# First x tile ahead of the weights, and activation sums rounded one unit sooner, in a one-core macaron decoder layer

## The chip, the core and the metric

The kernel runs on one NeuronCore of a Trainium2 chip. Its engines are TensorE (PE, with its weight loads shown apart as PEld), VectorE (DVE), ScalarE (ACT), GpSimd (POOL) and SyncE (SP), each with its own instruction stream; they meet only at semaphores. Loads from memory are issued on the queue of SP, and some on ACT's. The metric is the time of one execution in microseconds (us); less is better.

## What is computed

One layer of a decoder: a SwiGLU feed-forward, a mixer of two attention branches, and a second feed-forward, each between a norm ahead and a norm behind. The change lies in the two feed-forwards.

```python
def swiglu(x, w_gate, w_up, w_down):
    return (jax.nn.silu(x @ w_gate) * (x @ w_up)) @ w_down
...
    f1 = swiglu(rmsnorm(h, ffn1_pre_g[l]), ffn1_w_gate[l], ffn1_w_up[l], ffn1_w_down[l])
    h = h + 0.5 * rmsnorm(f1, ffn1_post_g[l])
...
    f2 = swiglu(rmsnorm(h, ffn2_pre_g[l]), ffn2_w_gate[l], ffn2_w_up[l], ffn2_w_down[l])
    h = h + 0.5 * rmsnorm(f2, ffn2_post_g[l])
```

There are 512 tokens, 1024 features and 2816 hidden features, all in float32.

## The kernel before

**Three products for one.** Each float32 operand is split in two: ACT writes a rounded copy (`w_hi`, `u_hi`, `a_hi`, and the first half of `tc`), DVE subtracts it from the original and writes the rest (`w_lo`, `u_lo`, `a_lo`, the second half of `tc`). PE then makes three matmuls: hi times hi, hi times lo, lo times hi. A unit is 128x1024 weights; four slots of `raw`, `w_hi` and `w_lo` go round.

**The start.** The first feed-forward starts from x transposed, in eight tiles of 128 features by 512 tokens (`xt`, which lies in `arena`). ACT makes `u_hi` of a tile with the gain `g1` (`u_tile`), DVE makes `u_lo` (`u_pair`). Units 0 and 1 are the first columns of w_gate and w_up. Each comes in two loads: the part for features 0 and 1 (`first_part(j, 0, 2)`, semaphore `w0_in[j]`) and the rest (`first_part(j, 2, KD)`). SP issues these four, then units 2 and 3 (`first_load`), then x in token order into `h`. ACT issues the gain and all of x transposed: tiles 0 and 1 one by one (L520), the other six in three loads of two (L522). All that stands ahead of ACT's first rounding (`first_hi(0)`, L706), which waits for `w0_in[0]`. PE goes by pairs of tiles (`earliest_units`, L1606 to L1612): for each of four pairs the six matmuls of unit 0 and the six of unit 1, so it needs tile pair n and, from pair 1 on, the rest of both weights. On ACT the order is first_hi(0), tiles 0 and 1, first_hi(1), rest_hi(0), tiles 2 and 3, rest_hi(1), tiles 4 to 7, units 2 and 3. Behind units 0 to 3 PE spreads the norm's factors with one matmul (L1622); ACT copies them (L652).

**The classic units and the pairs.** Units 0 to 7 are plain (`CLASSIC`); unit j is read from its bank by `silu` (ACT, L660) where j is even, with a scaling by DVE ahead of it in the first feed-forward (L1145), and by a product on DVE where j is odd (L1149, `hidden_ready`). Unit 6 takes the banks of unit 2, so PE waits for the second product of L1149 ahead of it. What follows are nine pairs (QP), each of seven units (STEPS) of half-size matmuls (L1534 to L1536): products of sums of weight blocks (DVE, L1047) and sums of activation blocks, from which the four wanted blocks are put together (`quads`, L1072). The activation sums are T_3, T_1, T_2 and T_4: DVE makes them in `token_sum` (L1129), ACT rounds them in `t_hi` (L643), DVE takes the rest in `t_lo` (L1105). They are made once for each feed-forward, and PE needs them from the second unit of the first pair on. Rounding a pair's weights is L604 on ACT, the rest L1053 on DVE.

**What sets the order.** Nothing is scheduled by a planner. Each engine's program is written out by hand, and an engine takes its rows in that order, each when its semaphores allow. In the loop over units 0 to 7 (`ffn` of ACT and of DVE) the token sums stand at units 0 to 3 and their rounding at units 4 to 7.

Of the kernel before, what the change touches and what calls it, by code (L numbers as in the profile page):

```python
# [23 lines left out]
P = 128  # L24
# [76 lines left out]
def macaron_layer(nc, h_store, x_t, g1cols, x, w1g, w1u, w1d, g1post, gmpre, w_in, b_forget, w_alpha, b_alpha,  # L101
                  gla_g, w_bf, w_bg, w_out, gmpost, g2pre, w2g, w2u, w2d, g2post, out):
    with ExitStack() as ctx:
# [295 lines left out]
        def _(sp):  # L399
# [45 lines left out]
            def first_part(j, k0, k1, done):  # L445
                src = kmajor((w1g, w1u)[j], slice(0, P))
                sp.dma_start(tiles(j)[:, k0:k1, :], src[:, k0:k1, :]).then_inc(done, 16)

            first_part(0, 0, 2, w0_in[0])
            first_part(1, 0, 2, w0_in[1])  # L450
            first_part(0, 2, KD, raw_in[0])
            first_part(1, 2, KD, raw_in[1])
# [59 lines left out]
        def _(act):  # L512
# [3 lines left out]
            act.wait_ge(bias_set, 1)  # L516
            nc.scalar.activation(ones[:, :], eps_t[:, :], ACT.Copy, scale=0.0, bias=1.0).then_inc(warm_set, 1)
            act.dma_start(g1[:, :], g1cols).then_inc(g1_in, 16)
            for k in range(2):
                act.dma_start(xt[:, k, :], x_t[k * P:(k + 1) * P, :]).then_inc(xt0_in[k], 16)  # L520
            for n in range(1, KD // 2):
                act.dma_start(xt[:, 2 * n:2 * n + 2, :],  # L522
                              x_t[2 * n * P:(2 * n + 2) * P, :].rearrange("(k p) c -> p k c", p=P)).then_inc(xt_in[n], 16)

            def split(u, i=0, per=0, second=None):

                act.wait_ge(raw_in[slot(u)], i * (16 * per // SLOTS) + arrivals(u))
                if second is not None:
                    act.wait_ge(*second)
                if not isinstance(i, int) or u + per * i >= SLOTS:  # L530
                    act.wait_ge(unit_used, i * per + (u - SLOTS + 1))
                nc.scalar.activation(w_hi[:, slot(u), :], raw[:, slot(u), :], ACT.Copy).then_inc(hi_ready, 1)  # L532
# [112 lines left out]
            def ffn(u0, layer):  # L645
                for j in range(4 * CLASSIC):
                    i, jj = j // 4, j % 4
                    if layer == 0 and j == 0:
                        split(u0 + 4)
                        split(u0 + 5)  # L650
                        act.wait_ge(rstd_spread, 1)
                        nc.scalar.activation(rstd_all, bank[:, 4, :], ACT.Copy).then_inc(rstd_kept, 1)  # L652
                    if jj % 2 == 0:
                        src = silu[:, jj // 2, :]
                        if layer:
                            act.wait_ge(unit_used, u0 + j + 1)
                            src = bank[:, classic_bank(layer, j), :]
                        else:
                            act.wait_ge(z_scaled, j // 2 + 1)
                        nc.scalar.activation(silu[:, jj // 2, :], src, ACT.Silu).then_inc(silu_ready, 1)  # L660
                    if i < CLASSIC - 1:
                        if layer:
                            split(u0 + j + 4)
                        elif jj % 2 == 0:
                            split(u0 + jj // 2 + 6)
                    else:
                        t_hi(layer, jj, (T_3, T_1, T_2, T_4)[jj])
                        pair_hi(layer, 0, jj)
                for q in range(QP):
                    for n in range(STEPS):  # L670
                        if q and n == 0:
                            silu_quads(layer, q - 1, 1)
                            silu_quads(layer, q - 1, 2)
                        if n == 1:
                            snapshot(layer, q, 0, y_pair(q))
                        if n == 2:
                            snapshot(layer, q, 1, w_pair)
                        if n == 3:
                            snapshot(layer, q, 2, y_pair(q))
                        if n == 5:  # L680
                            silu_quads(layer, q, 0)
                        if n == 0:
                            if q:
                                pair_hi(layer, q, 3)
                        elif n <= 3:
                            pair_hi(layer, q, n + 3)
                        elif q < QP - 1:
                            pair_hi(layer, q + 1, n - 4)
                        else:
                            down_hi(layer, n - 4)  # L690
                silu_quads(layer, QP - 1, 1)
                silu_quads(layer, QP - 1, 2)
                for n in range(3, KF):
                    down_hi(layer, n)
# [15 lines left out]
                nc.scalar.activation(w_hi[:, j, 2 * P:UNIT], raw[:, j, 2 * P:UNIT], ACT.Copy).then_inc(hi_ready, 1)  # L710

            first_hi(0)
            act.wait_ge(g1_in, 16)
            u_tile(0)
            u_tile(1)
# [223 lines left out]
        def _(dve):  # L939
# [191 lines left out]
            def ffn(u0, layer):  # L1131
                if layer:
                    for m in range(4):
                        token_whole(layer, m)
                for j in range(4 * CLASSIC):
                    i, jj = j // 4, j % 4
                    if layer == 0 and j == 0:
                        split(u0 + 4)
                        split(u0 + 5)
                        dve.wait_ge(rstd_kept, 1)  # L1140
                    if jj % 2 == 0 and layer == 0:
                        dve.wait_ge(unit_used, u0 + j + 1)
                        if i:
                            dve.wait_ge(hidden_ready, PAIRS + j // 2 - 1)
                        V.tensor_tensor(silu[:, jj // 2, :], bank[:, classic_bank(layer, j), :], rstd_all, ALU.mult).then_inc(z_scaled, 1)  # L1145
                    if jj % 2:
                        dve.wait_ge(unit_used, u0 + j + 1)
                        dve.wait_ge(silu_ready, 2 * CLASSIC * layer + j // 2 + 1)
                        V.tensor_tensor(arena[:, j // 2, :], silu[:, jj // 2, :], bank[:, classic_bank(layer, j), :],  # L1149
                                        ALU.mult).then_inc(hidden_ready, 1)  # L1150
                    if i < CLASSIC - 1:
                        if layer:
                            split(u0 + j + 4)
                        elif jj % 2:
                            split(u0 + jj // 2 + 6)
                        token_sum(layer, jj)
                        continue
                    t_lo(layer, jj, (T_3, T_1, T_2, T_4)[jj])
                    if jj == 0:
                        pair_sum_of(layer, 0, "S3")  # L1160
                        pair_sum_of(layer, 0, "S1")
                    pair_lo(layer, 0, jj)
                    if jj == 0:
                        pair_sum_of(layer, 0, "S2")
                    if jj == 3:
                        pair_sum_of(layer, 0, "S4")
                for q in range(QP):
                    last = q == QP - 1
                    for n in range(STEPS):
                        if n == 0 and q:  # L1170
                            if layer == 0:
                                quad_scale(q - 1, 2)
                            pair_lo(layer, q, 3)
                            pair_sum_of(layer, q, "S4")
                            quad_mul(layer, q - 1, 0)
                            quad_mul(layer, q - 1, 1)
                        if 1 <= n <= 3:
                            pair_lo(layer, q, n + 3)
                            if n == 1 and q:
                                quad_mul(layer, q - 1, 2)  # L1180
                            if n > 1 and not last:
                                pair_sum_of(layer, q + 1, ("S3", "S1")[n - 2])
                        if n >= 4:
                            quads(layer, q, n - 4)
                            if layer == 0 and n != 5:
                                quad_scale(q, n // 6)
                            if last:
                                down_lo(layer, n - 4)
                            else:
                                pair_lo(layer, q + 1, n - 4)  # L1190
                                if n == 4:
                                    pair_sum_of(layer, q + 1, "S2")
                if layer == 0:
                    quad_scale(QP - 1, 2)
                for n in range(3):
                    quad_mul(layer, QP - 1, n)
                for n in range(3, KF):
                    down_lo(layer, n)
# [738 lines left out]
```

## Time and profile before

| | us |
|---|---|
| median of 3 runs | 1090.79 |
| lowest, highest | 1090.13, 1091.5 |
| the profiled execution | 1090.27 |
| its span, first to last instruction | 1088.4 |
| PE busy | 1075.5 (99%) |
| PE weight loads busy | 957.5 (88%) |
| DVE busy | 667.9 (61%) |
| ACT busy | 503.0 (46%) |

1.9 us of the profiled execution lie outside its span, and it is 0.5 us below the median. The granted clock of TensorE is at full speed (2.4 GHz) in all of the 40 slices. PE is busy nearly throughout, so an edit can only give back one of PE's few gaps, or open one. Matmul ends are modelled, so a gap is best read from the start of a matmul behind a wait.

### The profile page before, as it was taken

To read this page: it belongs to the slowest core of one execution; us is meant where nothing else is said; L and a number is where in the kernel's file an instruction comes from. 1 tells how busy PE (TensorE), PEld (TensorE's weight loads), DVE (VectorE), ACT (ScalarE), POOL (GpSimd) and SP (SyncE) were. 2 spreads that over 40 slices of the span, in tenths; PEclk is the share of its full clock that TensorE was granted. 3 is DMA by queue.
4 is the path that set the end of the run, shared out by engine and by line. 5 is a ranking of instruction groups with operands and counts; after the bars stand their busy time and mean duration, and the time that the engine had idled before them with its cause. 6 is when DMAs were issued, how large, how long until landed. Compare 5 with 4: busy or idle time off the path is not lost.

```text
span 1088.4 us, 15986 instructions
## 1 busy us (share of the span) xinstructions
PE 1075.5 (99%) x6534; PEld 957.5 (88%) x6534; DVE 667.9 (61%) x810; ACT 503.0 (46%) x729; POOL 44.7 (4%) x96
## 2 busy tenths in 40 slices
PE   8999999999999999999999999999999999999997
PEld 6899999998888978888888888889899999988886
DVE  6898888873334663476664333468687887753334
ACT  7354455552223573667773222344445454542222
POOL 2000000000001210001000000011000000000001
PEclk9999999999999999999999999999999999999999
DMA  9522423334322544332115334315434234153311
GB/s 301 183 78 87 147 79 101 133 98 174 96 81 58 175 121 108 84 78 78 40 39 155 97 109 161 97 41 173 155 95 139 79 108 125 78 178 113 95 40 78
DMA packets 116131, 121.17 MB, mean 111 GB/s; under 512 B 6592, under 2 KB 100816, under 8 KB 116064
## 3 DMA queue, kind: packets, MB, share of 16 engines
q1 hardware_dynamic: 111744, 113.37, 33.8%
q10 hardware_dynamic: 3344, 4.20, 1.4%
q0 software_dynamic: 976, 2.66, 0.7%
q8 instruction: 47, 0.77, 0.3%
q14 instruction: 20, 0.16, 0.1%
HBM read 111.80 MB, written 6.29 MB: 108 GB/s over the span
## 4 chain that ended last, share of the span: by engine, by line
PE 90%; DVE 4%; ACT 3%; issue 1%; DMA 1%; POOL 0%; SPq 0%; ACTq 0%; DVEq 0%; POOLq 0%
PE bank L1448 25%; PE bank L1534 11%; PE bank L1536 11%; PE bank L1535 11%; PE bank L1438 7%; PE bank L1440 7%; PE bank L1439 7%; PE bank L1653 1%; PE bank L1654 1%; PE bank L1655 1%; PE bank L1503 1%; PE bank L1504 1%; PE bank L1505 1%; DMA raw<-in_ffn_w_up 1%; PE bank L1750 1%
## 5 line engine op out<-in xcount | busy, mean ns | idle before, releaser
L1534 PE MATMUL bank<-tc,w_hi 128*128 128x256 f32 x576 | 163.0, 283 | 0.0
L1535 PE MATMUL bank<-tc,w_hi 128*128 128x256 f32 x576 | 163.0, 283 | 0.0
L1536 PE MATMUL bank<-tc,w_lo 128*128 128x256 f32 x576 | 163.0, 283 | 0.0
L945 DVE TENSOR_TENSOR w_lo<-raw,w_hi 128x1024 fp32r<-128x1024 f32 x71 | 86.6, 1221 | 96.5 <-ACT w_hi L532 96.4
L1059 DVE TENSOR_TENSOR w_lo<-raw,w_hi 128x1024 fp32r<-128x1024 f32 x40 | 49.0, 1226 | 129.6 <-ACT w_hi L610 129.6
L1448 PE MATMUL bank<-w_hi,a_hi 128*128 128x512 f32 x408 | 126.1, 390 | 0.0
L1448 PE MATMUL bank<-w_hi,a_lo 128*128 128x512 f32 x408 | 125.7, 389 | 0.0
L1448 PE MATMUL bank<-w_lo,a_hi 128*128 128x512 f32 x408 | 125.6, 389 | 0.0
L1438 PE MATMUL bank<-u_hi,w_hi 128*128 128x512 f32 x312 | 124.0, 397 | 0.2 <-issue 0.2
L1534 PE MATMUL bank<-u_hi,w_hi 128*128 128x256 f32 x432 | 122.3, 283 | 0.8 <-DVE scr L1072 0.8
L1536 PE MATMUL bank<-u_hi,w_lo 128*128 128x256 f32 x432 | 122.2, 283 | 0.0
L1535 PE MATMUL bank<-u_lo,w_hi 128*128 128x256 f32 x432 | 122.2, 283 | 0.0
L1440 PE MATMUL bank<-u_hi,w_lo 128*128 128x512 f32 x312 | 121.8, 390 | 0.0
L1439 PE MATMUL bank<-u_lo,w_hi 128*128 128x512 f32 x312 | 121.6, 390 | 0.0
L1534 PEld LDWEIGHTS bank<-tc,w_hi 128*128 128x128 f32 x576 | 110.6, 192 | 0.0
L1535 PEld LDWEIGHTS bank<-tc,w_hi 128*128 128x128 f32 x576 | 110.6, 192 | 0.0
L1536 PEld LDWEIGHTS bank<-tc,w_lo 128*128 128x128 f32 x576 | 110.6, 192 | 0.0
L610 ACT ACTIVATE w_hi<-raw 128x1024 fp32r<-128x1024 f32 x40 | 42.4, 1060 | 141.6 <-PE bank L1448 137.9
L532 ACT ACTIVATE w_hi<-raw 128x1024 fp32r<-128x1024 f32 x71 | 74.7, 1054 | 56.0 <-PE bank L1440 24.3
L1448 PEld LDWEIGHTS bank<-w_lo,a_hi 128*128 128x128 f32 x408 | 76.6, 188 | 15.9
L1448 PEld LDWEIGHTS bank<-w_hi,a_lo 128*128 128x128 f32 x408 | 76.6, 188 | 15.9
L1448 PEld LDWEIGHTS bank<-w_hi,a_hi 128*128 128x128 f32 x408 | 76.1, 188 | 15.7 <-DVE arena L1408 0.2
(244 smaller groups left out, 2057.9 us busy)
## 6 DMA issues: line engine op xcount, KB each, us to landing
raw<-in_ffn_w_down SPq DMA_DIRECT2D x40, 512.0 KB, 3.6
raw<-in_w_in SPq DMA_DIRECT2D x40, 512.0 KB, 3.8
h<-in_ffn_w_gate SPq DMA_DIRECT2D x9, 1024.0 KB, 5.5
h<-in_ffn_w_up SPq DMA_DIRECT2D x9, 1024.0 KB, 8.5
raw<-in_ffn_w_gate SPq DMA_DIRECT2D x9, 1024.0 KB, 5.4
raw<-in_ffn_w_up SPq DMA_DIRECT2D x9, 1024.0 KB, 8.0
h<-in_x SPq DMA_DIRECT2D x8, 512.0 KB, 6.5
h_store<-h SPq DMA_DIRECT2D x2, 2048.0 KB, 9.3
```

Source lines behind the costliest of these rows:

```text
L532: nc.scalar.activation(w_hi[:, slot(u), :], raw[:, slot(u), :], ACT.Copy).then_inc(hi_ready, 1)
L610: nc.scalar.activation(w_hi[:, slot(u), :], raw_down(layer, n), ACT.Copy).then_inc(hi_ready, 1)
L945: V.tensor_tensor(w_lo[:, slot(u), :], raw[:, slot(u), :], w_hi[:, slot(u), :].bitcast(F32), ALU.subtract).then_inc(lo_ready, 1)
L1059: V.tensor_tensor(w_lo[:, slot(u), :], raw_down(layer, n), w_hi[:, slot(u), :].bitcast(F32), ALU.subtract).then_inc(lo_ready, 1)
L1438: mm(dst, w_hi[:, slot(u), w], rhs_hi[:, k - k0, :], start=k == k0, stop=False)
L1439: mm(dst, w_hi[:, slot(u), w], rhs_lo[:, k - k0, :], start=False, stop=False)
L1440: last = mm(dst, w_lo[:, slot(u), w], rhs_hi[:, k - k0, :], start=False, stop=k == k1)
L1448: last = mm(bank[:, 2 * t + c, :], a[:, s, toks], w[:, s, c * HALF:(c + 1) * HALF], start=first and a is a_hi and w is w_hi, stop=final an ...
L1503: mm(dst, w_hi[:, s, w], u_hi[:, k, toks], start=k == 0, stop=False)
L1534: mm(dst, w_hi[:, slot(u), w], moving(n, 0, k), start=first and k == 0, stop=False, skip_group_check=True)
L1535: mm(dst, w_hi[:, slot(u), w], moving(n, 1, k), start=False, stop=False, skip_group_check=True)
L1536: last = mm(dst, w_lo[:, slot(u), w], moving(n, 0, k), start=False, stop=k == KD // 2 - 1, skip_group_check=True)
```

## The change

The loads of x tiles 0 and 1 move from ACT's queue to SP's: tile 0 ahead of all weights, tile 1 behind the first part of w_gate. The three loads of the six later tiles stay on ACT's queue, but behind its first rounding. And the splits of the activation sums T_3, T_1 and T_2 move from units 4, 5 and 6 to units 1, 2 and 3, that of T_4 from unit 7 to unit 4, on ACT and on DVE, in both feed-forwards. No operation is added or taken away.

```diff
@@ sync
+            def first_rows(k):
+                sp.dma_start(xt[:, k, :], x_t[k * P:(k + 1) * P, :]).then_inc(xt0_in[k], 16)
+
+            first_rows(0)
             first_part(0, 0, 2, w0_in[0])
+            first_rows(1)
             first_part(1, 0, 2, w0_in[1])
             first_part(0, 2, KD, raw_in[0])
             first_part(1, 2, KD, raw_in[1])
@@ scalar
             act.dma_start(g1[:, :], g1cols).then_inc(g1_in, 16)
-            for k in range(2):
-                act.dma_start(xt[:, k, :], x_t[k * P:(k + 1) * P, :]).then_inc(xt0_in[k], 16)
-            for n in range(1, KD // 2):
-                act.dma_start(xt[:, 2 * n:2 * n + 2, :],
-                              x_t[2 * n * P:(2 * n + 2) * P, :].rearrange("(k p) c -> p k c", p=P)).then_inc(xt_in[n], 16)
...
                             split(u0 + jj // 2 + 6)
+                        if jj:
+                            t_hi(layer, jj - 1, (T_3, T_1, T_2)[jj - 1])
                     else:
-                        t_hi(layer, jj, (T_3, T_1, T_2, T_4)[jj])
+                        if jj == 0:
+                            t_hi(layer, 3, T_4)
                         pair_hi(layer, 0, jj)
...
             first_hi(0)
+            for n in range(1, KD // 2):
+                act.dma_start(xt[:, 2 * n:2 * n + 2, :],
+                              x_t[2 * n * P:(2 * n + 2) * P, :].rearrange("(k p) c -> p k c", p=P)).then_inc(xt_in[n], 16)
@@ vector
                         token_sum(layer, jj)
+                        if jj:
+                            t_lo(layer, jj - 1, (T_3, T_1, T_2)[jj - 1])
                         continue
-                    t_lo(layer, jj, (T_3, T_1, T_2, T_4)[jj])
                     if jj == 0:
+                        t_lo(layer, 3, T_4)
                         pair_sum_of(layer, 0, "S3")
                         pair_sum_of(layer, 0, "S1")
                     pair_lo(layer, 0, jj)
```

The first loads on SP's queue (`raw` is the weights, `arena` here x transposed):

```order
 L398 UNCONDITIONAL_BRANCH
+L450 DMA arena<-in_x_t 128x512
 L447 DMA raw<-in_ffn_w_gate 128x2x128
+L450 DMA arena<-in_x_t 128x512
 L447 DMA raw<-in_ffn_w_up 128x2x128
 L447 DMA raw<-in_ffn_w_gate 128x6x128
```

Two loads came in ahead, so each load behind them is issued one or two places later.

ACT at the start, before:

```order
L518 DMA g1<-in_g1_cols 128x8
L520 DMA arena<-in_x_t 128x512 x2
L522 DMA arena<-in_x_t 128x2x512 x3
L706 ACTIVATE w_hi<-raw 128x256
L702 ACTIVATE u_hi<-arena,g1 128x512 x2
```

and after:

```order
L523 DMA g1<-in_g1_cols 128x8
L709 ACTIVATE w_hi<-raw 128x256
L717 DMA arena<-in_x_t 128x2x512 x3
L705 ACTIVATE u_hi<-arena,g1 128x512 x2
```

The three loads of x now stand behind the rounding that waits for the first part of w_gate, and still ahead of the first two tiles' rounding.

DVE in the first feed-forward, from the scaling of unit 0 to the first pair's first sum, before:

```order
L1145 TENSOR_TENSOR scr<-bank,scr 128x512
L1129 TENSOR_TENSOR arena<-arena 128x1024
L1149 TENSOR_TENSOR arena<-scr,bank 128x512
L945 TENSOR_TENSOR w_lo<-raw,w_hi 128x1024
L1129 TENSOR_TENSOR arena<-arena 128x1024
L1145 TENSOR_TENSOR scr<-bank,scr 128x512
L1129 TENSOR_TENSOR arena<-arena 128x1024
L1149 TENSOR_TENSOR arena<-scr,bank 128x512
L945 TENSOR_TENSOR w_lo<-raw,w_hi 128x1024
L1129 TENSOR_TENSOR arena<-arena 128x1024
L1145 TENSOR_TENSOR scr<-bank,scr 128x512
L1105 TENSOR_TENSOR tc<-arena,tc 128x1024
```

and after, where the line numbers are 6 higher (L1111 is `t_lo`, L1151 the scaling, L1155 the product):

```order
L1151 TENSOR_TENSOR scr<-bank,scr 128x512
L1135 TENSOR_TENSOR arena<-arena 128x1024
L1111 TENSOR_TENSOR tc<-arena,tc 128x1024
L1155 TENSOR_TENSOR arena<-scr,bank 128x512
L951 TENSOR_TENSOR w_lo<-raw,w_hi 128x1024
L1135 TENSOR_TENSOR arena<-arena 128x1024
L1111 TENSOR_TENSOR tc<-arena,tc 128x1024
L1151 TENSOR_TENSOR scr<-bank,scr 128x512
L1111 TENSOR_TENSOR tc<-arena,tc 128x1024
L1053 TENSOR_TENSOR scr<-h 128x1024
```

This piece begins at the scaling of unit 2. One t_lo stands ahead of that scaling (T_3), one between the second token sum behind it and the product (T_1), one ahead of the scaling of unit 4 (T_2), and T_4's behind it.

## Rows read from the trace of the kernel before

**Rows 1.** The page's first line.
```profile
span 1088.4 us, 15986 instructions
```
**Rows 2.** Waits of PE, whole span: who for whom, us, times, longest.
```profile
PE bank L1606 <- ACT u_hi L702: 1.6, 2, 0.8
```
**Rows 3.** The chain that ended last, at the start: start us, us, what.
```profile
2.31 9.20 DMA raw<-in_ffn_w_up
```
**Rows 4.** Timeline, 0 to 16 us: start us, us, engine, line, operation, [idle before].
```profile
0.81 0.43 SPq L447 DMA_DIRECT2D raw<-in_ffn_w_gate  x1
...
2.40 1.85 ACTq L522 DMA_DIRECT2D arena<-in_x_t  x3
...
3.48 3.79 SPq L414 DMA_DIRECT2D raw<-in_ffn_w_up  x1
...
9.64 1.34 ACT L702 ACTIVATE u_hi<-arena,g 128x512 fp32r<-128x512 f32 x2 [1.12 <-DMA arena<-in_x_t]
...
10.51 1.02 PE L1606 MATMUL bank<-u_hi,w_hi 128*128 128x512 f32 x2
...
14.46 0.62 PE L1606 MATMUL bank<-u_hi,w_hi 128*128 128x512 f32 x2
```
**Rows 5.** DMA queues, 0 to 6.8 us: packets, MB, share. q1 is SP's, q10 ACT's.
```profile
q1 hardware_dynamic: 1643, 0.82, 44.4%
q10 hardware_dynamic: 450, 0.57, 23.3%
```
**Rows 6.** DMA queues, 7 to 9 us.
```profile
q10 hardware_dynamic: 287, 0.56, 79.9%
q1 hardware_dynamic: 297, 0.15, 28.0%
```
**Rows 7.** Issue to landing: first part of w_gate, of w_up (both L447), and L522.
```profile
DMA to landing us min/median/max: 2.3/2.3/2.3
...
DMA to landing us min/median/max: 3.6/3.6/3.6
...
DMA to landing us min/median/max: 7.2/8.5/9.8
```
**Rows 8.** Timeline, 16 to 18 us: small constants on ACT's queue, SP's next weights.
```profile
16.33 0.54 ACTq L726 DMA_DIRECT2D bias_small<-in_b_forget  x1
...
17.95 3.44 SPq L407 DMA_DIRECT2D raw<-in_ffn_w_gate  x1
```
**Rows 9.** DMA queues, 20.5 to 22.5 us.
```profile
q10 hardware_dynamic: 782, 0.00, 26.2%
```
**Rows 10.** Timeline of DVE, 26 to 80 us.
```profile
35.96 1.22 DVE L1129 TENSOR_TENSOR arena<-arena 128x1024 f32<-128x1024 f32 x1
37.09 0.69 DVE L1145 TENSOR_TENSOR scr<-bank,scr 128x512 f32<-128x512 f32 x1
37.69 1.22 DVE L1129 TENSOR_TENSOR arena<-arena 128x1024 f32<-128x1024 f32 x1
...
44.04 1.23 DVE L1105 TENSOR_TENSOR tc<-arena,tc 128x1024 fp32r<-128x1024 f32 x1 [1.65 <-ACT tc L643]
...
55.23 1.23 DVE L1105 TENSOR_TENSOR tc<-arena,tc 128x1024 fp32r<-128x1024 f32 x1 [1.65 <-ACT tc L643]
...
60.57 1.23 DVE L1047 TENSOR_TENSOR h<-h 128x1024 f32<-128x1024 f32 x1
...
70.91 0.68 DVE L1072 TENSOR_TENSOR scr<-scr,bank 128x512 f32<-128x512 f32 x1
```
**Rows 11.** Timeline of ACT, 26 to 80 us.
```profile
42.42 0.63 ACT L660 ACTIVATE scr<-scr 128x512 f32<-128x512 f32 x1 [3.03 <-DVE scr L1145]
42.96 1.04 ACT L643 ACTIVATE tc<-arena 128x1024 fp32r<-128x1024 f32 x1
```
**Rows 12.** Timeline of PE at unit 6's first matmul, and in the first pair.
```profile
42.57 0.39 PE L1438 MATMUL bank<-u_hi,w_hi 128*128 128x512 f32 x1
...
71.64 0.38 PE L1534 MATMUL bank<-u_hi,w_hi 128*128 128x256 f32 x1 [0.76 <-DVE scr L1072]
```

## The prediction

> **What bounds the kernel.** I read the table of busy time, then PE's waits, then the chain that ended last, and then the timelines of the two places that the change touches. PE is busy for 99% of a span of 1088.4 us [rows 1], at full clock, so DVE or ACT counts only where PE waits for it. PE's waits are few; of those at the places of the change the largest in the list are 1.6 us for ACT's first rounded x tiles [rows 2] and 0.76 us in the first pair [rows 12]. At the start the chain runs through one load: the rest of w_up, issued at 2.31 and under way for 9.20 us [rows 3]. From the matmul at 14.46 [rows 4] PE has no gap until the first pair, so whatever moves that matmul moves the end. I sum against the profiled execution (1090.27 us: the span and 1.9 us around it) and put the sum on the median, which is 0.5 us higher.
>
> **Loads at the start, what the rows show.** The first pair of x tiles that rides on the later loads is rounded at 9.64, PE begins on it at 10.51, 0.87 behind, and comes to the second pair at 14.46 [rows 4], 3.95 behind its start. Six matmuls for each of two units at 0.227 us apiece are 2.7 us, so 1.2 us of that are waits. The rest of w_up lands at 11.51 and takes ACT and DVE three quarters of a full step each, some 1.8 us in all with the hand-overs, so its lo part is there at 13.4, where PE would want it at 12.6 to 12.8: 0.6 to 0.8 of the 1.2. The other 0.45 are the tiles' own roundings. The load of that pair was issued at 2.40 [rows 4] and landed 7.2 us later, at 9.60 [rows 7]. Its bytes came late: by 6.8 us ACT's queue had moved 450 packets [rows 5]. The gain (128 rows and 16 closing packets) and tiles 0 and 1 (256 and 32) are 432 of those, so the third load began only around 6.8, 4.4 us behind its issue, and needed 2.8 us from there to landing. By then SP's queue had moved 1643 packets [rows 5] of the 2048 rows of 512 bytes that its first four loads hold. I read this as one generator of descriptors that serves both queues in the order of issue: ahead of that load stood SP's 2048 rows and ACT's 384, 2432 in some 4.9 us, about 500 per us. A second place agrees: small constants issued by ACT from 16.33 on, while SP was held up, moved their 782 packets only at 20.5 to 22.5, and they did get ahead of what SP issued at 17.95 [rows 8, 9].
>
> **Tiles 0 and 1 to SP.** SP's first issue is at 0.81 and its fourth at 2.31 [rows 3, 4], so a place costs 0.50 us. Two more places put the load of unit 2 from 2.9 to about 3.9 and that of unit 3 to 4.45. The first part of w_gate is issued at 1.3 and has tile 0 ahead. Before, it landed 2.3 us behind its issue as the first on the queue; the first part of w_up, second on the queue, took 3.6 [rows 7]. So it now lands between 3.6 and 4.9; I take 4.2, since tile 0 brings twice its bytes ahead of it but half the rows. Tile 0 itself comes sooner, but ACT reaches it only behind three issues (1.85 us in all [rows 4]), at about 6.0; PE's work on tiles 0 and 1 ends about 11, ahead of what follows, and costs nothing.
>
> **The six later tiles.** They are issued when that part lands, at about 4.2, in place of 2.40. By then SP has issued unit 2 (1024 rows) too, so ahead of the first of them stand 2432 and 1024 rows: its bytes begin 2.05 us later, at 8.85, and it lands 2.8 behind that, at 11.6. PE then begins on it at 12.5. The wait for the rest of w_up is gone, since SP's queue runs alone until 8.85 and that load lands near 8. So from there to the next pair are 2.7 and 0.45 us: 15.65 in place of 14.46, **1.2 us later**. Later tiles follow at 1.9 us a pair against PE's 2.7 and hide. The weights of unit 2 hide too. SP's loads behind unit 3 wait for room on the queue as they did; those of the first pair are wanted only around the step at 44.04 [rows 10].
>
> The Trainium skill ("DMA: Bandwidth & Descriptors", "Issuing engines are not separate DMA queues") holds that issuing from SP and from ACT runs on the same engines and saves only the time of the issue. Taken alone that speaks against a gain from the move of tiles 0 and 1 and prices the wait for ACT's later issue at its 1.8 us, less what hides; the rows above put 2.05 in that place.
>
> **Splits one unit sooner, first feed-forward.** ACT and DVE do the same work, in another order, and DVE has no gap there. A full-size step takes 1.14 us from start to start (35.96 to 37.09) and a half-size one 0.60 (37.09 to 37.69) [rows 10]; on ACT a next one starts some 0.09 before the last ends (42.42 and 0.63 against 42.96, 1.04 for a full one) [rows 11]. From the token sum at 35.96, which stays: t_lo of T_3 stands at 37.10, the scaling of unit 2 at 38.24 (before 37.09), the next token sum at 38.84. ACT, which waited for the scaling, does silu at 38.96, the split of unit 7 at 39.50, t_hi of T_1 at 40.45 to 41.49. DVE waits for that in place, idle 1.55 us, and only then takes the product of unit 3, at 42.67 to 43.35. PE wants that product at 42.57 [rows 12], for unit 6. It stalls until 43.40: **a new wait of 0.8 us**. DVE goes on with the split of unit 7 at 43.27, the last token sum, t_lo of T_2, and the scaling of unit 4 at 46.69. ACT does silu and t_hi of T_4 at 47.41 and 47.95, so DVE starts t_lo of T_4 at 49.03. Before, the t_lo in that place stood at 44.04 [rows 10]: 4.99 later. Three of 1.14 us no longer follow, 3.42; the wait of 1.65 ahead of the step at 55.23 [rows 10] stays, since ACT still does silu and one full rounding, now of weights, between. So the last sum of the first pair moves from 60.57 to 62.1, and what follows it without a gap moves as much: the quad at 70.91 [rows 10], for which PE waits at 71.64 [rows 12], ends near 73.1. PE's wait there was 0.76; with the 0.8 lost ahead it is about 1.2, with 0.3 at the pair's third unit. **The sum is +1.5 us**, as the DVE chain and not PE sets it. The bounds: -0.76, if neither wait is left; +2.4, if PE's new wait for unit 6 were paid beside the chain.
>
> **Second feed-forward, 0.** The last classic split on DVE comes some 1.7 us later there, and with it the loads of the first pair, but PE has no wait in that stretch, before or behind it, and the first pair's roundings run more than 1.7 us ahead of PE. That lead is the cover.
>
> Sum: 1.2 and 1.5 are 2.7 on 1090.27, which is 1093.0 for the profiled execution, and **1093.4** on the median, 0.24% slower.
>
> **The rivals.** (a) The part of w_gate lands before 3.9, so ACT's later tiles get in ahead of unit 2: their bytes begin at 6.8 as before, and the start gains the 0.8 us of the rest of w_up. With 1.5 that is +0.7: **1091.5**, no change. The 3.6 speaks for it, the 4.9 against. (b) It lands behind 4.45, and unit 3's 1024 rows stand ahead too: again 2.05 us, so +4.7: **1095.5**. (c) ACT's requests don't wait for SP's. Then the later tiles flow from about 5.5, and share. Between 7 and 9 us both queues moved as many packets, 287 and 297, but ACT's of 0.56 MB against 0.15 [rows 6]. By 6.8 both had moved 1.39 MB [rows 5], by 5.5 at the same pace about 0.95; the four weight loads and tiles 0 and 1 are 1.57. So some 0.6 MB are left on SP's queue, which gets 0.075 MB/us for the 5.5 us of ACT's 1.57 MB, and the rest of w_up lands at 12.2 to 13.2 where it landed at 11.5: +0.7 to +1.7, **1093.5**. The Trainium skill (same page, "Queues, rings and completion order") says that an engine takes turns between the queues by packet; by this rule the trace agrees. (d) Only the splits don't do what I say: DVE, lighter by three steps in the first pair, is early, and the 0.76 goes, with no wait at unit 6. With the start at +1.2 that is **1091.2**. (e) Faster: all x and weights come in the order of use. PE's eight groups up to unit 2 are 10.9 us; before, they end at 14.46 and 5.44, 19.9. Run without a gap from the time at which ACT has tile 0 rounded, about 6.3, they would end at 17.2, a gain of 2.7; with -0.76 end at **1087.4**. It decides the sign if the first pair of later tiles lands before 8. Against it speaks that they are issued later and nothing ahead of them has gone.
>
> **How the numbers follow.** My forecast has 0.35, (a) 0.19, (b) 0.17, (c) 0.13, (d) 0.08, (e) 0.08. 0.2% is 2.2 us and about what a measurement of this kernel can tell from no change. Slower by more (over 1093.0): 0.25 of my forecast's, all of (b), 0.10 of (c): 0.52. Faster by more: (e), 0.08. Within: 0.40. The range runs from 1090.4, which takes in (a) and (d) with 0.8 of error below, to 1096.0 above (b); it leaves (e) and some of the tails out.
>
> **What would show it.** First feed-forward: a PE gap of 0.8 us at unit 6's first matmul for a DVE product, DVE idle 1.5 us ahead of the second t_lo, and PE's wait in the pair's seventh unit grown to about 1.2. If PE shows no gap at unit 6, (d) holds. Start: the landing of the first of the three ACT loads, 11.6 in my forecast, 9.6 in (a), 13.6 in (b); the rest of w_up near 8, and past 12 in (c). PE's matmul of the second later pair at 15.65.

## The result, and the profile after

| | before | after |
|---|---|---|
| median, us | 1090.34 (13 runs) | 1093.32 (13 runs) |
| ratio, 95% interval | | 1.0027 [1.0018, 1.0035] |
| the profiled execution | 1090.27 | 1093.36 |
| its span | 1088.4 | 1091.5 |

One of the 13 executions of the kernel before took 1307.36 us, all others between 1089.65 and 1091.50, and the median hardly feels it. The changed kernel is slower by 3.0 us. Both of its halves cost something, and each at the place that the prediction named. The page's first line, to be read beside [rows 1]:

```profile
span 1091.5 us, 15986 instructions
```

PE's waits, of which these four touch the change (before they were 1.6, nothing, 0.8 and nothing, [rows 2, 12]). A row says who waited for whom, the us in total, the times, and the longest:

```profile
PE bank L1614 <- ACT u_hi L705: 2.5, 2, 1.4
...
PE bank L1542 <- DVE scr L1078: 0.9, 1, 0.9
...
PE bank L1446 <- DVE arena L1155: 0.7, 1, 0.7
...
PE bank L1542 <- ACT scr L623: 0.2, 1, 0.2
```

The timeline of the start, answering to [rows 4]:

```profile
3.79 0.55 SPq L414 DMA_DIRECT2D raw<-in_ffn_w_gate  x1
4.17 0.42 ACT L709 ACTIVATE w_hi<-raw 128x256 fp32r<-128x256 f32 x1 [1.87 <-DMA raw<-in_ffn_w_gate]
4.18 1.77 ACTq L717 DMA_DIRECT2D arena<-in_x_t  x3
4.38 2.87 SPq L414 DMA_DIRECT2D raw<-in_ffn_w_up  x1
...
11.90 1.33 ACT L705 ACTIVATE u_hi<-arena,g 128x512 fp32r<-128x512 f32 x2 [3.14 <-DMA arena<-in_x_t]
...
12.76 1.02 PE L1614 MATMUL bank<-u_hi,w_hi 128*128 128x512 f32 x2 [1.03 <-ACT u_hi L705]
...
16.08 0.62 PE L1614 MATMUL bank<-u_hi,w_hi 128*128 128x512 f32 x2
```

ACT's three loads are issued at 4.18, between the issues of units 2 and 3. The first of them landed 7.7 us later, at 11.88, and PE's second later pair of tiles began at 16.08 where it was 14.46: the start costs **1.62 us**. What the two queues moved from 7 to 9 us (q1 is SP's, q10 ACT's), where ACT's had moved 0.56 of the 0.71 MB before [rows 6]:

```profile
q1 hardware_dynamic: 1062, 0.53, 102.7%
q10 hardware_dynamic: 38, 0.08, 11.8%
```

ACT's copy of the norm's factors is the last event that only the start decides. It came at 33.45, 1.61 after the 31.84 of before. The row of before, and the one after:

```profile
31.84 0.60 ACT L652 ACTIVATE scr<-bank 128x512 f32<-128x512 f32 x1 [5.22 <-PE bank L1622]
...
33.45 0.60 ACT L652 ACTIVATE scr<-bank 128x512 f32<-128x512 f32 x1 [6.29 <-PE bank L1630]
```

From there on the splits count. DVE, first feed-forward, answering to [rows 10]; L1111 is the rest of an activation sum (`t_lo`), here of T_3, T_1 and T_4:

```profile
38.70 1.22 DVE L1111 TENSOR_TENSOR tc<-arena,tc 128x1024 fp32r<-128x1024 f32 x1
39.84 0.68 DVE L1151 TENSOR_TENSOR scr<-bank,scr 128x512 f32<-128x512 f32 x1
...
43.12 1.23 DVE L1111 TENSOR_TENSOR tc<-arena,tc 128x1024 fp32r<-128x1024 f32 x1 [1.46 <-ACT tc L643]
44.26 0.68 DVE L1155 TENSOR_TENSOR arena<-scr,bank 128x512 f32<-128x512 f32 x1
...
50.59 1.23 DVE L1111 TENSOR_TENSOR tc<-arena,tc 128x1024 fp32r<-128x1024 f32 x1 [1.65 <-ACT tc L643]
```

and the three places at which PE waits, answering to [rows 12]: unit 6's first matmul, and the first pair's third and seventh units:

```profile
45.00 0.50 PE L1446 MATMUL bank<-u_hi,w_hi 128*128 128x512 f32 x1 [0.66 <-DVE arena L1155]
...
62.11 0.39 PE L1542 MATMUL bank<-tc,w_hi 128*128 128x256 f32 x1 [0.19 <-ACT scr L623]
...
74.81 0.39 PE L1542 MATMUL bank<-u_hi,w_hi 128*128 128x256 f32 x1 [0.93 <-DVE scr L1078]
```

From the copy to the first matmul of the pair's seventh unit before took 71.64 - 31.84 = 39.80 us, after 74.81 - 33.45 = 41.36: the splits cost **1.56 us**. 1.61 and 1.56 make 3.17 us; the span grew by 3.1. This distance, 39.80 before, is the measure in what follows: it holds nothing of the start.

### The profile page after: what moved, and what is told of

The parts are those of the page before. It is cut to its first block, busy times and chain, and to the rows that moved or that the text cites. A ratio compares the mean times of both kernels' runs of the same rounds, so it can differ in the third digit from the quotient of the medians.

```text
span 1091.5 us, 15986 instructions
## 1 busy us (share of the span) xinstructions
PE 1077.1 (99%) x6534; PEld 958.8 (88%) x6534; DVE 668.0 (61%) x810; ACT 503.0 (46%) x729; POOL 44.6 (4%) x96
## 4 chain that ended last, share of the span: by engine, by line
PE 85%; DVE 5%; ACT 3%; issue 2%; POOL 0%; ACTq 0%; DVEq 0%; POOLq 0%
PE bank L1456 25%; PE bank L1542 11%; PE bank L1543 11%; PE bank L1544 11%; PE bank L1446 6%; PE bank L1448 6%; PE bank L1447 6%; PE bank L1661 1%; PE bank L1662 1%; PE bank L1663 1%; PE bank L1511 1%; PE bank L1512 1%; PE bank L1513 1%; PE bank L1758 1%; DVE w_lo L1059 1%
```

## The experiments

Each kernel ran in 11 executions (the last in 7) beside the kernel before on the same chip. Its median there was 1090.3 in the first two groups of runs and 1090.5 in the third. An interval is about 0.9 us to each side, as wide as most of the effects, so each verdict on a mechanism goes by the trace of one execution, and the median says whether the size agrees.

**The loads alone**: the splits as before.

```diff
+            first_rows(0)
             first_part(0, 0, 2, w0_in[0])
+            first_rows(1)
...
             first_hi(0)
+            for n in range(1, KD // 2):
+                act.dma_start(xt[:, 2 * n:2 * n + 2, :],
```

> Only the loads of the change, with the splits as before. Theory A (the first pair of later x tiles waits behind 1024 rows of unit 2 that SP queued first, and the two parts of the change add up): the first pair of later tiles lands about 11.9 us, ACT copies the norm's factors 1.6 us later than before (33.45 for 31.84), PE's wait in the first pair stays at 0.76, total +1.6 us, 1092.0. Rival B (the loads cost less, and part of the delay comes from the two parts meeting): total +0.5 us or less.

1091.73 us, ratio 1.0012 [1.0003, 1.0021]. The chain that ended last and the row behind it:

```profile
4.19 8.17 DMA arena<-in_x_t
```
```profile
12.38 1.33 ACT L702 ACTIVATE u_hi<-arena,g 128x512 fp32r<-128x512 f32 x2 [3.19 <-DMA arena<-in_x_t]
```

Same instructions and the same time of issue as in the changed kernel, but this execution's load took 8.17 us. The copy came at 33.95, and from there to the seventh unit it was 39.80 again, as before. So the loads cost the start alone, 2.1 us in this execution and 1.4 in the median.

**The splits alone**: all loads as before.

```diff
+                        if jj:
+                            t_hi(layer, jj - 1, (T_3, T_1, T_2)[jj - 1])
...
+                        if jj:
+                            t_lo(layer, jj - 1, (T_3, T_1, T_2)[jj - 1])
```

> Only the splits of the activation sums, with the loads as before. Theory A (DVE has no gap there, and waits once more for ACT): PE gap of 0.7 to 0.8 us at unit 6, about 0.9 to 1.2 in the first pair's seventh unit, from the copy of the norm's factors to that seventh unit 41.4 us in place of 39.8; total +1.5 us, 1091.9. Rival B (the splits only show a wait that the late start caused): from copy to seventh unit 39.8, total +0.2 or less.

1091.87 us, 1.0016 [1.0007, 1.0025]. PE:

```profile
43.32 0.50 PE L1443 MATMUL bank<-u_hi,w_hi 128*128 128x512 f32 x1 [0.66 <-DVE arena L1152]
```
```profile
73.11 0.39 PE L1539 MATMUL bank<-u_hi,w_hi 128*128 128x256 f32 x1 [0.91 <-DVE scr L1075]
```

The copy stands at 31.78, as before, and the distance is 41.33. The same three waits, without the loads: +1.5 us by the distance, 1.57 by the medians. With the 1.43 of the loads alone that makes 3.0, the whole cost: within what the intervals can tell the two halves add.

**Units 2 and 3 held back** until ACT has rounded tile 0, on top of the loads alone.

```diff
             first_part(1, 2, KD, raw_in[1])
+            sp.wait_ge(u0_hi, 1)
             first_load(2)
             first_load(3)
```

> As the loads-only kernel, but SP holds the loads of units 2 and 3 until ACT has rounded x tile 0, so that at the issue of the later tiles (about 4.2) only the 2432 rows stand ahead of them, as before the change. Splits as before. Theory A (one generator takes requests of both queues in the order of issue, about 500 rows per us): the first pair of later tiles lands at 9.7 to 10.2, 5.6 to 6 us behind its issue in place of 7.7. Rival C (the delay is of ACT's queue itself, or the time of issue sets it): it lands 7.7 us behind its issue, near 11.9, as in the loads-only kernel. In A the rest of w_up then shares with the tiles and lands near 12, so the total is between +0.2 and +1.0 us on before; in C +1.6.

1090.45 us, 1.0002 [0.9993, 1.0011]. The chain, and PE's second later pair:

```profile
4.15 6.30 DMA arena<-in_x_t
```
```profile
14.66 0.62 PE L1610 MATMUL bank<-u_hi,w_hi 128*128 128x512 f32 x2
```

This is the run that shows the mechanism. ACT issued at the same time as in the two kernels with the loads (4.15, 4.18, 4.19), its load was the same, and only the 2048 rows of units 2 and 3 no longer stood on SP's queue ahead of it or beside it: it landed 6.3 us later and not 7.7 or 8.2, and the cost of the start is gone from the median. What ACT's load waits for is on another engine's queue. From 7 to 9 us the queues moved here:

```profile
q1 hardware_dynamic: 603, 0.30, 56.6%
q10 hardware_dynamic: 170, 0.35, 50.2%
```

The prediction let the load begin where 18 packets of x had gone, behind the gain's 144. Counted so, it began at about 8.0 here and 8.6 in the changed kernel, and then took 2.45 us here and 3.25 there, with 56 of SP's packets moved meanwhile here and 651 there. So of the 1.43 us between the two landings some 0.6 lie ahead of the load's bytes, and some 0.8 are turns taken with SP's rows. It is no strict order of issue: in the changed kernel unit 2's load was issued at 3.79, ahead of ACT's, and landed at 14.5, 2.6 us behind it.

Two numbers missed: the landing, at 10.45, was 0.25 us later than the latest I had expected, and the rest of w_up landed at 9.1 and not near 12.

**All x tiles on SP's queue, in the order of use**: tile 0, w_gate's first part, tile 1, w_up's first part, the rest of w_gate, tiles 2 and 3, the rest of w_up, tiles 4 to 7, and then units 2 and 3. Splits as before.

```diff
             first_part(0, 2, KD, raw_in[0])
+            rows_pair(1)
             first_part(1, 2, KD, raw_in[1])
+            rows_pair(2)
+            rows_pair(3)
             first_load(2)
```

> All x tiles on SP's queue in the order of use: tile 0, first part of w_gate, tile 1, first part of w_up, rest of w_gate, tiles 2 and 3, rest of w_up, tiles 4 and 5, 6 and 7, then units 2 and 3. Splits as before. Theory A (the start is bound by the order in which bytes come, and a single queue is a plain line): tiles 2 and 3 land about 8.6, the rest of w_up about 10.2, PE comes to tiles 4 and 5 at 13.0 for 14.46; total -1.4 us, 1088.9. Rival (the bytes up to the last tile bound it, in whatever order): no change, within 0.4 us.

1089.28 us, 0.999 [0.9981, 0.9999], faster than the kernel before. Its chain, and its wait in the pair's seventh unit:

```profile
3.21 6.02 DMA arena<-in_x_t
```
```profile
70.68 0.39 PE L1541 MATMUL bank<-u_hi,w_hi 128*128 128x256 f32 x1 [0.76 <-DVE scr L1079]
```

The load is issued later than before (3.21 and not 2.40) and lands sooner, at 9.23. The copy is at 30.89, 0.95 us sooner. So it was not the place of tile 0 that cost, but that the six later tiles were left behind units 2 and 3. The gain fell short of the 1.4 us expected: the load was to land at 8.6, and PE came to tiles 4 and 5 at 13.48 and not 13.0.

**The splits of the second feed-forward alone.** The edit is shown against the splits alone, for DVE; on ACT it is the same condition, and the first feed-forward keeps its order of before.

```diff
-                        if jj:
+                        if jj and layer:
                             t_lo(layer, jj - 1, (T_3, T_1, T_2)[jj - 1])
```

> The splits of the activation sums one unit sooner in the second feed-forward alone; the first feed-forward and the start are those of the kernel before. The prediction put the price there at 0. Theory A (PE has no wait there, and the first pair's roundings run more than 1.7 us ahead of it): the time of before within its noise, 1090.3 us, and no new wait of PE behind the second feed-forward's classic units. Theory B (DVE's idle time ahead of the second rest and the later product hold unit 6 as in the first feed-forward): a gap of 0.3 to 0.8 us there, 1090.6 to 1091.1 us.

1090.49 us, 1.0004 [0.9995, 1.0013], span 1088.6, and 39.81 from the copy to the seventh unit. No wait of PE was added to the list. The prediction's 0 there holds within the 1 us that the runs can tell.

**T_1's rest behind the product of unit 3**, on top of the splits alone.

```diff
                         ALU.mult).then_inc(hidden_ready, 1)
+                        if j == 3:
+                            t_lo(layer, 1, T_1)
...
-                        if jj:
+                        if jj in (1, 3):
                             t_lo(layer, jj - 1, (T_3, T_1, T_2)[jj - 1])
```

> As the kernel with the splits alone moved, but DVE takes the rest of T_1 behind the product of unit 3 and not ahead of it, so that it does not wait for ACT's rounding with a finished product's inputs at hand. Theory A (the cost of the move is made of a gap of some 0.66 us at unit 6 and a wait in the seventh unit grown by some 0.2 with 0.2 at the third, all from DVE's idle time ahead of T_1's rest): no gap at unit 6; DVE idle about 1.0 us in place of 1.5; PE's waits in the first pair are then 1.3 to 1.7 us in all where they were 0.76: +0.6 to +0.95, 1090.9 to 1091.3 us. Theory B (the cost is all in the gap, and with it gone nothing is late): 1090.3 us. Theory C (the length of the DVE chain sets the end whatever stands ahead of the product, so the whole cost stays): 1091.8 us.

Median 1092.28 us, 1.0015 [1.0006, 1.0024], above the range of each of the three theories; alone it would say that nothing was gained. The trace says otherwise:

```profile
33.23 0.60 ACT L652 ACTIVATE scr<-bank 128x512 f32<-128x512 f32 x1 [6.62 <-PE bank L1629]
```
```profile
61.29 0.39 PE L1541 MATMUL bank<-tc,w_hi 128*128 128x256 f32 x1 [0.44 <-ACT scr L623]
...
73.98 0.39 PE L1541 MATMUL bank<-u_hi,w_hi 128*128 128x256 f32 x1 [0.93 <-DVE scr L1075]
```

PE has no gap at unit 6 any more, and the distance is 40.75: +0.95, the upper end of what I expected of a shorter DVE idle time. The rest is the start, which this kernel doesn't touch and which was 1.4 us late in this execution. Its executions lie at 1090.9 to 1091.3 (four, 0.6 to 0.9 above before) and at 1092.05 to 1092.84 (seven); the run on PE's warming, below, takes that up. The four agree with the trace's 0.95. Why seven of 11 lie higher here, where 7 of the 33 of the kernel before do, is not shown. So by the trace most of the splits' cost stays without the gap: DVE is still idle for 0.87 us ahead of T_1's rest, and its later waits for ACT stay.

**The first two activation sums ahead of DVE's wait for the norm's factor**, where it stood idle.

```diff
                         split(u0 + 5)
+                        for m in range(2):
+                            token_sum(layer, m)
                         dve.wait_ge(rstd_kept, 1)
...
-                        token_sum(layer, jj)
+                        if layer or jj >= 2:
+                            token_sum(layer, jj)
```

> The kernel before, but DVE makes the first two of the first feed-forward's four activation sums ahead of its wait for the norm's factor, where it stood idle from about 29.6 to 32.4 us, and not among the classic units. Nothing else is moved. Theory A (what PE waits for in the first pair is the length of DVE's chain from the factor's arrival to that pair's sums, whatever is in it): two steps of 1.14 us no longer lie in that chain, so PE's wait of 0.76 us in the pair's seventh unit goes, and nothing replaces it: 1090.3 - 0.76 = 1089.6 us. Theory B (DVE waits for ACT further on, at 1.65 us ahead of the step at 55.23, and this resets the chain): the gain of 2.3 us is used up there as a longer wait, and the pair's last sum comes as late as before: 1090.3 us.

1089.48 us, 0.9996 [0.9987, 1.0005]. DVE, and then ACT's copy:

```profile
29.53 2.35 DVE L1129 TENSOR_TENSOR arena<-arena 128x1024 f32<-128x1024 f32 x2
33.69 0.69 DVE L1147 TENSOR_TENSOR scr<-bank,scr 128x512 f32<-128x512 f32 x1 [1.81 <-ACT scr L652]
35.15 0.69 DVE L1151 TENSOR_TENSOR arena<-scr,bank 128x512 f32<-128x512 f32 x1 [0.77 <-ACT scr L660]
```

PE's wait in the seventh unit is gone from the list, and from the copy to that unit it is 38.88 us for 39.80. From DVE's first scaling to T_3's rest it is 10.43 us where it was 11.57: of the 2.28 us taken out 1.14 are back as waits, 0.77 for ACT's silu among them.

**One sum ahead.** The first one moves as above, and the second takes its place.

```diff
+                        token_sum(layer, 0)
                         dve.wait_ge(rstd_kept, 1)
...
-                        token_sum(layer, jj)
+                        if layer or jj != 1:
+                            token_sum(layer, jj if layer or jj else 1)
```

> The kernel before with the first activation sum alone ahead of the wait for the norm's factor. Theory A: DVE's chain is 1.14 us shorter, PE's wait of 0.76 in the first pair's seventh unit goes: 1089.6 us, copy of the factor to the seventh unit's first matmul 39.0 us where it was 39.8. Theory B (chain reset further on): 1090.3 us.

1089.36 us against 1090.48, 0.9994 [0.9985, 1.0003]. PE's wait is gone in this one too, and the distance is 38.88 again, with DVE idle for 1.48 us ahead of the scaling: one sum does what two did.

**Sums and loads together.** The loads in the order of use, with their diff above, and two sums ahead, with theirs:

> Both edits that should help: all x tiles on SP's queue in the order of use with the weights of units 0 and 1, and the first two activation sums ahead of DVE's wait for the norm's factor. Theory A (the two gains lie at different places and add): -1.0 and -0.76 us, 1088.6 us, with PE's first wait at tiles 2 and 3 and none in the first pair's seventh unit. Theory B (with PE about 1 us earlier, DVE's sums start later against it, since the factor comes from x in token order behind all these loads, and the second gain is used up): 1089.3 us.

1089.40 us, 0.9991 [0.9982, 1.0], no better than the loads alone. DVE and PE:

```profile
30.04 2.36 DVE L1136 TENSOR_TENSOR arena<-arena 128x1024 f32<-128x1024 f32 x2
32.31 0.69 DVE L1154 TENSOR_TENSOR scr<-bank,scr 128x512 f32<-128x512 f32 x1
33.76 0.69 DVE L1158 TENSOR_TENSOR arena<-scr,bank 128x512 f32<-128x512 f32 x1 [0.77 <-ACT scr L667]
```
```profile
70.35 0.39 PE L1544 MATMUL bank<-u_hi,w_hi 128*128 128x256 f32 x1 [0.60 <-DVE scr L1079]
```

The factor's copy, at 30.71, was ready at 31.3, while DVE was in its second sum until 32.3. The idle time had shrunk, by 1.1 us since the copy came sooner and by 0.5 since DVE's splits ahead of the sums ended later (30.04 for 29.53), and no longer held two sums. The distance is 39.64, so only 0.16 of the 0.92 us of the sums was left. The gains didn't add, as the second of the two theories said.

Then the same loads with one sum ahead:

> All x tiles on SP's queue, and only the first activation sum ahead of DVE's wait for the norm's factor, the second in the first one's old place. With both sums ahead DVE came to the factor 1.0 us after its copy, and then stood 0.77 us for ACT's silu: of 2.28 us only 1.14 were left. Theory A (one sum fits into the idle time, which ends at about 31.2 us, and saves the same 1.14): no wait of PE in the first pair's seventh unit, 0.76 less than with the loads alone, 1088.5 us. Theory B (DVE's chain is reset by its 1.65 us wait for ACT further on): the wait stays, 1089.3 us.

**1088.70 us, 0.9983 [0.9974, 0.9992]**, the shortest median of all. There is no wait left in the seventh unit, and the distance is 38.88:

```profile
31.11 1.22 DVE L1136 TENSOR_TENSOR arena<-arena 128x1024 f32<-128x1024 f32 x1
32.55 0.69 DVE L1153 TENSOR_TENSOR scr<-bank,scr 128x512 f32<-128x512 f32 x1 [0.21 <-ACT scr L659]
```

That is 1.8 us below the kernel before, where the loads in the order of use alone gave 1.0 and one sum alone 1.1. The profiled execution shows only the sum's part: its first later load took 7.13 us and landed at 10.33, and the copy came at 31.91, no sooner than before. That one sum fits and two do not with the copy at 30.7 is read from DVE's rows; the medians of the two kernels, 1088.70 and 1089.40, have intervals that overlap.

Of the change this kernel keeps tile 0 ahead of all weights and tile 1 behind the first part of w_gate, and drops the rest.

**Ten warming matmuls in place of eight**, on the kernel before. The executions of the kernel before fall into two groups some 1.1 us apart: in this group of runs 23 of 29 were at 1090.84 or less and 6 at 1091.29 or more.

```diff
-WARM = 8
+WARM = 10
```

> The kernel before with ten and not eight of the matmuls on constants that stand ahead of PE's first product, so that PE is busy to about 6.2 us, when tile 0 is rounded, and not idle from 5.5. In the profiles PE's first products came at 0.43 us a matmul up to about 13 in some executions (1.2 GHz) and at 0.23 in others, and those with 0.43 ended 1.2 to 1.4 us later; the runs of the kernel before fall into 1090.3 and, less often, 1091.5. Theory A (PE's pause ahead of the first products decides which): hardly a run near 1091.5 is left, median 1090.2 us, and the products at 0.23 from the first. Theory B (the pause has nothing to do with it): the same two groups in the same proportion, 1090.3 us.

1090.00 us, 0.9995 [0.9986, 1.0004], and none of 11 above 1090.81. In the profile PE still paused, for 0.30 us where it was 0.75, and its products came at the full pace. With 6 in 29 one would expect two late ones in 11; that none came happens by chance once in ten times or so, so this speaks for the pause of PE as the cause and doesn't settle it.

**Twelve warming matmuls** on the changed kernel.

```diff
-WARM = 8
+WARM = 12
```

> The changed kernel with twelve and not eight matmuls on constants, so that PE is busy to about 7.0 us, when its tile 0 is rounded. In its profile the first two tiles' products came at 0.43 us a matmul up to 10.6. Theory A (that slow stretch ends well ahead of 12.76, where PE waits for the first later pair in any case, and is hidden): 1093.3 us. Theory B (the lower clock carries on behind that wait, and part of the start's +1.6 us is the clock's): 0.4 to 1.2 us less, 1092.1 to 1092.9 us.

1093.37 us, 1.0031 [1.0019, 1.0042].

```profile
11.05 1.34 ACT L705 ACTIVATE u_hi<-arena,g 128x512 fp32r<-128x512 f32 x2 [2.17 <-DMA arena<-in_x_t]
```
```profile
11.92 1.02 PE L1614 MATMUL bank<-u_hi,w_hi 128*128 128x512 f32 x2 [1.60 <-ACT u_hi L705]
...
15.23 0.63 PE L1614 MATMUL bank<-u_hi,w_hi 128*128 128x512 f32 x2
```

The warming ended at 6.2, since its last matmuls ran at the higher clock, and PE paused 0.68 us. It went at full pace from 7.7 on (where the changed kernel's products came 0.43 us apart to 10.6) and only waited longer for the first later pair (1.60 and not 1.03). From its start to the next pair it is 3.31 us here and 3.32 in the changed kernel. The slower stretch of that one's profile, 6.93 to 10.6, cost nothing. The load landed sooner in this execution, 7.1 us behind its issue, which is the load's own spread.

## Why the prediction was right, point by point

**The total.** 1093.4 was forecast and 1093.32 measured, but part of that is luck: the sum was +2.7 and came out +3.0, while the median of before that I put it on was, over more runs, 0.45 us lower. (1090.79 and 2.7 are 1093.49, so the 1093.4 has a slip of 0.1.)

**The place of ACT's later loads** held. w_gate's first part landed at 4.15 (forecast 4.2), between the issues of units 2 and 3. The load's bytes were to begin at 8.85, and by the count of 18 packets they did at about 8.6. But the fixed pace of 500 rows per us is not borne out: with units 2 and 3 held back the same 2432 rows stood ahead as before, and the load began at about 8.0 and not at 6.8. By 6.8 the two queues had moved 2093 packets before and 1733 in the changed kernel. Nor did all rows of unit 2 go ahead of the load; a good part of them took turns with it. Rival (a) wanted the landing before 3.9, (b) a first load at 13.6; neither came. Rival (c), requests that don't wait and share, wanted the rest of w_up past 12.2; it landed at 9.2. Of its two halves the first fell, since ACT's requests did wait; the second, sharing, holds once the load has begun. The run with units 2 and 3 held back brought the load in sooner by nothing but an emptier queue of SP's. The Trainium skill ("DMA: Bandwidth & Descriptors", "Issuing engines are not separate DMA queues") has the choice of issuing engine save only the time of issue. Taken as a price, that would put the first later load 1.8 us later in both of these kernels. It was 0.85 later with units 2 and 3 held (10.45 for 9.60) and 2.28 later in the changed kernel, so the measurement decides for what stands on SP's queue.

**The start's size** was too small: 1.2 forecast, 1.62 in the profile. The mechanism held and two terms were mis-sized: "it lands 2.8 behind that, at 11.6" and "2.7 and 0.45 us". From its 18th packet the load took 3.25 us and not 2.8, since it shared with SP's rows, and landed at 11.88; and the pair took 3.32 us and not 3.15. I had also said that the rest of w_up would land near 8; it took till 9.2, which cost nothing. In three executions of these same loads the first later load landed at 11.03, 11.88 and 12.36, and the second pair began 0.8, 1.6 and 2.1 us late; the median of the loads alone is +1.4. One profile could not have told 1.2 from 1.6.

**The splits** held step by step. T_3's rest was forecast at 37.10, the scaling at 38.24, the product's end at 43.35 and T_4's rest at 49.03; less the start's 1.61, they stood at 37.09, 38.23, 43.33 and 48.98. DVE's idle time was 1.46 (1.55), the sum 1.56 (1.5). The distribution over PE's waits needs a correction. A listed wait begins at the modelled end of the last matmul, 0.28 or 0.39 us behind its start, while the next one would have started after 0.12 or 0.23; and the first matmul behind a wait takes another 0.10. Counted from start to start, the 0.76 of before is 71.64 - 70.60 - 0.12, and 0.10 more, that is 1.02 us. After, the three are 0.93, 0.45 and 1.19, in all 2.57, and 2.57 - 1.02 is the 1.55 that the distance shows. That also is why taking the wait of 0.76 away gave 1.1 us: the span with one sum ahead is 1.6 shorter than before, 0.54 of it from the start.

**Rival (d)**, the splits doing no harm, fell with the gap at unit 6. **Rival (e)**, all in the order of use, is not what the change does, and its speed came only when the six tiles stood ahead of units 2 and 3: 1.0 us of the 2.7 that it was worked out to at most.

**The second feed-forward** cost nothing, as said.

## What to carry to other kernels

Moving a load to another engine's queue doesn't take it out of line: ask which rows of all queues are requested ahead of it or move beside it, and put everything that is wanted first on one queue in the order of use. A split that waits for another engine must not stand ahead of a step that is ready and that a third engine wants. And work moved into idle time fills it only as long as that time lasts: with the start 1.1 us sooner, two sums no longer fitted.

## What the runs showed of the hardware

**The lower clock at the start.** In some executions PE's first products of 128x512 came 0.43 us apart, in others 0.23: with T_1 moved 0.43 up to 13.4, in the kernel before 0.23 from 7.9 on. A row of the kernel with two sums ahead, two matmuls in 1.05 us, where that takes 0.62 at the full pace:

```profile
9.18 1.05 PE L1615 MATMUL bank<-u_lo,w_hi 128*128 128x512 f32 x2
```

In the run with the second feed-forward alone the granted clock of that pace can be read: 0.55 from 8 to 10 us and 0.60 from 10 to 12, near the lower of the two levels (1.2 GHz). The first of these rows is of the kernel before, the second of that run; the column behind POOL's is the clock:

```profile
8.00:10.00 2.00, 2.00 (x10) 1.47 (x9) 1.52 (x3) 0.88 (x2) 0.00 (x0) 1.00 1.07 359
```
```profile
8.00:10.00 2.00, 2.00 (x6) 1.49 (x6) 1.70 (x3) 0.90 (x2) 0.00 (x0) 0.55 1.08 363
```

In other executions at that pace (two sums ahead, T_1 moved, the changed kernel) this column said 1.00, so it is the spacing of matmuls that tells it. Ahead of the slow stretch PE had paused between its warming matmuls, which end at 5.2 to 5.5, and its first product, 0.6 to 1.4 us; in the profile of before it had paused too, 0.75 us, and kept its pace. The Trainium skill ("TensorE: Matmul & The Clock Gate", "What's actually happening") says that the length of the cold stretch varies from run to run; here it does. What it costs depends on its end: where it lasted to about 13 and PE wasn't held up by a load, the copy of the factor came 1.2 and 1.4 us later (33.06 and 33.23 for 31.84); where it ended by 11.6, in the run with the second feed-forward alone, 0.23 later (32.07); and in the changed kernel, where it ended at 10.6 ahead of a wait, it cost nothing that shows.

**One load, three durations.** The same load, issued at 3.96, 4.18 and 4.19, took 7.1, 7.7 and 8.2 us in three executions. In the shortest SP issued unit 3 at 4.53, 0.57 us behind ACT, and in the other two at 4.38, 0.2 behind, which fits fewer of unit 3's rows beside it but is not tested; between 7.7 and 8.2 SP's issues start at the same times. ACT's issue of the three loads took 1.92, 1.77 and 2.15 us, in no order that explains it. With all x tiles on SP's queue the first later load, issued at 3.20 or 3.21, took 5.9, 6.0 and 7.1 us in its three executions. Such a spread is as large as most effects here, and one profile alone would mislead.
